# Six up projections of a two-block transformer as seven block products for eight

## The reference

```
h2 = rms_norm(x, norm2[l])
x = x + jnp.square(jax.nn.relu(h2 @ w_up[l])) @ w_down[l]
...
FFN_HIDDEN = math.ceil(8 * D_MODEL / 3 / 256) * 256
...
def swiglu_ffn(x, w_gate_up, w_down):
    gu = x @ w_gate_up
    gate, up = gu[..., :FFN_HIDDEN], gu[..., FFN_HIDDEN:]
    return (jax.nn.silu(gate) * up) @ w_down
```

## Time and profile before

| | us |
|---|---|
| median of 3 runs (2246.28 to 2247.21) | 2246.77 |
| the profiled execution | 2248.02 |
| its span, first to last instruction | 2246.3 |
| TensorE busy | 2184.9 |
| VectorE busy | 1036.7 |
| ScalarE busy | 842.4 |
| GpSimd busy | 243.5 |

### The profile page before, as it was taken

How to read it: one execution, slowest core, us unless ns; L and a number is a source line. 1 busy time by engine, 2 the same in 40 slices (tenths; PEclk the granted TensorE clock), 3 DMA queues, 4 the chain that set the end, 5 groups by cost and what they waited for, 6 DMA issues and landing times.

```text
span 2246.3 us, 34926 instructions
## 1 busy us (share of the span) xinstructions
PE 2184.9 (97%) x14575; PEld 1791.7 (80%) x14575; DVE 1036.7 (46%) x1704; ACT 842.4 (38%) x1480; POOL 243.5 (11%) x327
## 2 busy tenths in 40 slices
PE   8999999999999999988999999999999999999998
PEld 7777778888888887867878888888976779888887
DVE  5243436454344345556547443333535555333335
ACT  5354444342232235234334323222446644222231
POOL 4000000000000011102314100000422214000000
PEclk9999999999999999989999999999999999999999
DMA  5312123233333323200013233333232212333321
GB/s 171 85 57 57 48 67 103 85 94 94 99 98 94 85 86 85 76 21 2 3 30 100 83 115 94 96 96 100 69 82 67 71 47 83 106 103 103 93 86 65
DMA packets 341336, 179.65 MB, mean 80 GB/s; under 512 B 44151, under 2 KB 332069, under 8 KB 341181
## 3 DMA queue, kind: packets, MB, share of 16 engines
q1 hardware_dynamic: 338860, 171.54, 27.2%
q0 software_dynamic: 2320, 5.89, 0.9%
HBM read 172.40 MB, written 2.11 MB: 78 GB/s over the span
## 4 chain that ended last, share of the span: by engine, by line
PE 45%; DVE 2%; POOL 1%; ACT 1%; issue 1%; DMA 0%; DVEq 0%; POOLq 0%; ACTq 0%
PE bank L462 13%; PE bank L464 13%; PE bank L463 13%; PE bank L1405 2%; PE bank L1431 1%; PE bank L1417 1%; POOL x L1063 0%; ACT w_hi L438 0%; PE bank L923 0%; PE bank L2933 0%; POOL act_lo L972 0%; PE bank L2941 0%; DVE w_lo L445 0%; DMA mla_swapped<-mla_qr 0%; DVE o L967 0%
## 5 line engine op out<-in xcount | busy, mean ns | idle before, releaser
L462 PE MATMUL bank<-act_hi,w_hi 128*128 128x512 f32 (+1 forms) x1960 | 737.0, 376 | 10.5 <-DVE w_lo L445 3.3
L464 PE MATMUL bank<-act_hi,w_lo 128*128 128x512 f32 (+1 forms) x1960 | 714.6, 365 | 0.0
L463 PE MATMUL bank<-act_lo,w_hi 128*128 128x512 f32 (+1 forms) x1960 | 714.4, 364 | 0.0
L445 DVE TENSOR_TENSOR w_lo<-w,w_hi 128x1024 fp32r<-128x1024 f32 (+2 forms) x327 | 400.2, 1225 | 404.5 <-ACT w_hi L438 404.3
L438 ACT ACTIVATE w_hi<-w 128x1024 fp32r<-128x1024 f32 (+1 forms) x328 | 336.6, 1028 | 342.2 <-PE bank L464 326.6
L462 PEld LDWEIGHTS bank<-act_hi,w_hi 128*128 128x128 f32 x1960 | 370.7, 189 | 84.2 <-issue 17.5
L464 PEld LDWEIGHTS bank<-act_hi,w_lo 128*128 128x128 f32 x1960 | 370.7, 189 | 60.1
L463 PEld LDWEIGHTS bank<-act_lo,w_hi 128*128 128x128 f32 x1960 | 371.4, 190 | 53.7 <-issue 1.0
L462 PE MATMUL bank<-hid_hi,w_hi 128*128 128x512 f32 (+1 forms) x672 | 249.5, 371 | 0.0
L463 PE MATMUL bank<-hid_lo,w_hi 128*128 128x512 f32 (+1 forms) x672 | 247.9, 369 | 0.0
L464 PE MATMUL bank<-hid_hi,w_lo 128*128 128x512 f32 (+1 forms) x672 | 247.8, 369 | 0.0
(11 more groups left out here) (440 smaller groups left out, 2352.4 us busy)
## 6 DMA issues: line engine op xcount, KB each, us to landing
w<-in_ffn_w_gate_up SPq DMA_DIRECT2D x88, 512.0 KB, 3.8
w<-in_w_in SPq DMA_DIRECT2D x41, 512.0 KB, 3.8
w<-in_w_up SPq DMA_DIRECT2D x32, 512.0 KB, 4.0
w<-in_w_down SPq DMA_DIRECT2D x32, 512.0 KB, 3.8
w<-in_ffn_w_down SPq DMA_DIRECT2D x32, 512.0 KB, 3.9
w<-in_even_w_in SPq DMA_DIRECT2D x28, 512.0 KB, 3.8
w<-in_ffn_w_down SPq DMA_DIRECT2D x16, 384.0 KB, 3.4
w<-in_w_out SPq DMA_DIRECT2D x8, 512.0 KB, 3.9
```

The lines of the kernel that those rows point to most:

```text
L445: e.tensor_tensor(w_lo[:, 0:part.n], w.raw[part.g % w.LOADS][:, 0:part.n], w_hi[:, 0:part.n].bitcast(F32), ALU.subtract).then_inc(w.lo.sem, 1)
L462: e.matmul(s.acc, *first, start=(k == 0), stop=False)
L463: e.matmul(s.acc, *second, start=False, stop=False)
L464: last = e.matmul(s.acc, *third, start=False, stop=(k == kt - 1))
```

## The change

Six up jobs are computed by another rule: `up1`, `up2`, `up3` (squared ReLU) and `up01`, `up02`, `up11` (gated). Two tiles of output are taken as a pair. The pair's product is a matrix product of 2 x 2 blocks: the weight's blocks are a11, a12 (first tile, input features 0 to 511 and 512 to 1023), a21, a22 (second tile), the activation's are 512 features x 256 tokens, b11 to b22. Winograd's form of Strassen's rule needs seven block products where the plain one needs eight:

- sums of the activation, t1 = b12 - b11, t2 = b22 - t1, t3 = b22 - b12, t4 = b21 - t2, made once for each norm's result by GpSimd, split by ScalarE and VectorE (`scalar_after`, `vector_after`);
- sums of the weight, s1 = a21 + a22, s2 = s1 - a11, s3 = a11 - a21, s4 = a12 - s2, made for each pair by GpSimd, four additions of 128 x 512;
- seven products, each of 4 x 3 matmuls of 256 columns;
- results joined: ScalarE copies product 1 out of PSUM (`kept`), VectorE makes four additions with one input in PSUM, three of 512 columns and one of 256, into `z` in SBUF. The epilogue then reads `z` and not a bank, so its work on the pair's two tiles starts behind the fourth addition.

The weight parts of a pair are now a (a11, a12: 1024 columns), b (s2, s1), c (s3, s4) and d (a22, 512 columns), so four splits of 3584 columns in all where two of 2048 were. Loads stay two for a pair; the first buffer is free when the fourth sum and the split of a are made, the second when the split of d is made. In the jobs above TensorE runs 84 matmuls of 256 columns for a pair instead of 48 of 512; 36 pairs are changed.

The core of the diff:

```diff
+    def gpsimd(self, e):
...
+        s2, s1, s3, s4 = (self.S[:, n * T:(n + 1) * T] for n in range(4))
+        for s in self.subs:
+            pair, i = s.pair, s.pair.i
+            (a11, a12), (a21, a22) = pair.blocks()
+            if before:
+                e.wait_ge(*w.sums.at(4 * i))
+                e.wait_ge(*w.lo.at(before.parts[1].g + 1))
...
+            e.wait_ge(*w.landed_at(pair.loads[1]))
+            e.tensor_tensor(s1, a21, a22, ALU.add).then_inc(w.sums.sem, 1)
+            e.wait_ge(*w.landed_at(pair.loads[0]))
+            e.wait_ge(*w.sums.at(4 * i + 1))
+            e.tensor_tensor(s2, s1, a11, ALU.subtract).then_inc(w.sums.sem, 1)
+            if before:
+                e.wait_ge(*w.lo.at(before.parts[2].g + 1))
+            e.tensor_tensor(s3, a11, a21, ALU.subtract).then_inc(w.sums.sem, 1)
+            e.wait_ge(*w.sums.at(4 * i + 2))
+            e.tensor_tensor(s4, a12, s2, ALU.subtract).then_inc(w.sums.sem, 1)
+            before = pair
...
+        def product(acc, part, at, x):
...
+            w_hi, w_lo = g.split_of(part)
+            for k in range(4):
+                high, low = x(k)
+                cols = slice(at * T + k * P, at * T + (k + 1) * P)
+                e.matmul(acc, w_hi[:, cols], high, start=k == 0, stop=False)
+                e.matmul(acc, w_hi[:, cols], low, start=False, stop=False)
+                last = e.matmul(acc, w_lo[:, cols], high, start=False, stop=k == 3)
+            return last
...
+        e.wait_ge(*w.lo.at(a.g + 1))
+        room(0)
+        product(p1, a, 0, plain(0, first)).then_inc(w.made.sem, 1)
+        room(1)
+        product(p2, a, 1, plain(1, first)).then_inc(w.used.sem, 1)
+        e.wait_ge(*w.lo.at(b.g + 1))
+        product(p6, b, 0, sums(1)).then_inc(w.made.sem, 1)
+        room(2)
+        product(p5, b, 1, sums(0)).then_inc(w.used.sem, 1)
+        e.wait_ge(*w.lo.at(c.g + 1))
+        product(p7, c, 0, sums(2)).then_inc(w.made.sem, 1)
+        room(3)
+        product(p3, c, 1, plain(1, second)).then_inc(w.used.sem, 1)
+        e.wait_ge(*w.lo.at(d.g + 1))
+        product(p4, d, 0, sums(3)).then_inc(w.used.sem, 1)
+
+    def emptied(self, i, n):
+
+        w = self.w
+        return (w.kept.at(i + 1), w.added.at(4 * i + 1), w.added.at(4 * i + 3), w.added.at(4 * i + 4))[n]
...
+        e.wait_ge(*w.made.at(3 * i + 2))
+        e.wait_ge(*w.kept.at(i + 1))
+        e.tensor_tensor(z[:, 0:5:4, :], p2_p6, spread(self.kept[:, :], 2), ALU.add).then_inc(w.added.sem, 1)
+        for old in s.carried + [a]:
+            for part in g.next_of(old):
+                g.split_low(e, part)
+        e.wait_ge(*w.made.at(3 * i + 3))
+        e.wait_ge(*w.added.at(4 * i + 1))
+        e.tensor_tensor(z[:, 5:7, :], p5_p7, spread(z[:, 4, :], 2), ALU.add).then_inc(w.added.sem, 1)
+        e.wait_ge(*w.added.at(4 * i + 2))
+        e.tensor_tensor(z[:, 3, :], p5_p7[:, 0, :], z[:, 6, :], ALU.add).then_inc(w.added.sem, 1)
+        for part in g.next_of(b):
+            g.split_low(e, part)
+        e.wait_ge(*w.used.at(d.g + 1))
+        e.tensor_tensor(z[:, 1:3, :], p3_p4, z[:, 5:7, :], ALU.add).then_inc(w.added.sem, 1)
...
         for c, (first, n) in enumerate(CHUNKS):
...
+            if layer == 0 and c or layer and c == 1:
+                jobs[f"up{layer}{c}"] = SevenJob(w, f"up{layer}{c}", 2 * n, KD, pieces)
```

More of the change, by code:

```diff
@@ L235, in load, with loads_before @@
                 dst = dst.rearrange("p k (h n) -> p (k h) n", n=src.shape[-1])
[L236 to L242, removed]
+            e.dma_start(dst, src).then_inc(self.landed[n % self.LOADS].sem, 16)
+    def loads_before(self, e, n):
+        n = min(n, len(self.loads))
+        for i in range(self.issued, n):
+            self.load(e, i)
+        self.issued = max(self.issued, n)
 class Job:
@@ L273, in factors, with __init__, bind_seven, starts @@
         return (w_hi[:, at:at + P], hi), (w_hi[:, at:at + P], lo), (w_lo[:, at:at + P], hi)
+class SevenJob(Job):
+    def __init__(self, weights, name, tiles, kt, pieces):
+        self.name, self.tiles, self.kt, self.group = name, tiles, kt, 1
+        self.pairs = [weights.add_pair(kt, pieces(u), pieces(u + 1)) for u in range(0, tiles, 2)]
+        self.parts = [part for pair in self.pairs for part in pair.parts]
+    def bind_seven(self, seven):
+        self.seven = seven
+        for pair in self.pairs:
+            pair.seven = seven
+    def starts(self, u, k):
+        return None
+    def ends(self, u, k):
+        return None
 class TokenJob(Job):
@@ L359, in __init__ @@
             s.n, s.acc, s.before = n, self.bank[b][:, s.cols], before.get(b)
-            before[b] = s
+            if s.pair is None:
+                before[b] = lambda s=s: s.job.epilogue.emptied(self, s)
+            elif s.group:
+                four = [(n + i) % self.BANKS for i in range(4)]
+                s.banks, s.befores = [self.bank[b] for b in four], [before.get(b) for b in four]
+                for i, b in enumerate(four):
+                    before[b] = lambda s=s, i=i: s.job.seven.emptied(s.pair.i, i)
             found[s.job, s.u, s.cols.start, s.cols.stop] = s
@@ L369, in __init__ @@
                         part.ended_in = leader.n + -(-leader.group * (k + 1) // s.job.kt) - 1
-            if not s.ends[-1]:
+            if s.pair and s.group:
+                s.last = n + 2 == len(self.subs) or self.subs[n + 2].pair is None
+                s.carried = self.subs[n - 1].pair.parts[2:] if self.subs[n - 1].pair else []
+                for k, part in enumerate(s.pair.parts):
+                    part.ended_by, part.ended_in = n + 1 if s.last and k >= 2 else None, None
+            elif not s.pair and not s.ends[-1]:
                 partial += 1
@@ L495, in _ @@
             for s in self.subs:
-                if s.group:
+                if s.pair and s.group:
+                    s.job.seven.multiply(e, s, between)
+                elif s.group:
                     self.multiply(e, self.subs[s.n:s.n + s.group], between)
```

248 lines of the change are left out of this document (211 added, 37 removed).

## The result

The changed kernel takes 2269.2 us (median of 4 runs, 2268.49 to 2274.29), the kernel before 2247.0: 1.0101 times as long, 95% interval 1.0085 to 1.0117. The forecast was 2258, +11; it came to +22. The profiled execution is the longest of the four (2274.3, span 2272.3), so its parts add up to 26.0 us, not to 22.

What follows compares the result with a forecast made beforehand. TensorE's matmul columns bound the kernel while splits, sums and epilogues keep ahead. Three ReLU chunks at +2.0 and three gated at +1.6 give +10.8 on 2248.0, 1.3 less for the median: forecast 2258 us, range 2230 to 2276, its own 2250 to 2267.

Steps and rivals of the forecast that it cites:

- Matmuls at 0.12: On TensorE, 256-column matmuls start every 0.12 us, so seven products take 10.08 us against 10.88 before.
- The wait of 0.3 ahead of the second product: In gated pairs from the fourth on, TensorE gaps of about 0.3 us before product 2, released by a VectorE addition.
- Late: 1.75 - 0.9 = 0.85: In a gated pair, GpSimd holds VectorE 1.75 us against 0.9 slack, so the next pair's first product waits 0.85 us.
- The slack: In a gated pair, VectorE reaches add 3 in 4.9 us, TensorE needs it after 5.76: 0.9 us spare.
- the restart: After a gated pair's wait, TensorE loses 0.07 us more on starting again.
- The gated chunk: Up job of eight gated pairs: -1.6 + 5 x 0.55 - 0.5 + 0.9 = +1.6 us.
- the free pairs: First two pairs of a chunk save 0.80 us each, their sums being made during the down tiles.
- The hidden tile out late: Behind a chunk's last pair, the down job waits for the hidden tile: 0.9 us gated (0 to 1.5), ReLU 1.7.
- The ReLU chunk as a whole: Four pairs: two free (-1.6), third +2.4, last -0.5, hidden tiles 1.7 late: +2.0 us.
- The input sums at 0 to 3: Activation sums on GpSimd and their splits, during the up*0 jobs and first down tiles: 0, at most 3 us per stage.
- "The rest" at 0: Outside the chunks: input sums, load issue and GpSimd's later work were counted as adding 0.
- Rival C: GpSimd's chain of split, load and four additions sets the pair at 12.1 us: +25, total 2272; chance 0.17.

Runs made afterwards that it cites:

- last two narrow: Changed kernel with GpSimd's third and fourth weight sums cut to 8 of 512 columns from a stage's second pair on: 2234.9 us, ratio 0.9943.
- last-pair run: Changed kernel with the last pair of each of the six chunks computed as two plain tiles again: 2254.8 us, ratio 1.0027.
- first two pairs: Changed kernel with only the first two pairs of each of the six chunks as seven products, the rest plain: 2243.4 us, ratio 0.9986.
- ReLU chunks alone: Changed kernel with only the three squared ReLU chunks as seven products, the gated ones as before: 2259.3 us, ratio 1.0055.

## Why the prediction was wrong

The direction and most places were right, the size was not: +22.2 against +10.8, and the forecast's own range ended at 2267.

- **Matmuls at 0.12**: right, slightly better (9.96 for a pair against 10.08). First three gated pairs without a wait, waits from the fourth on, released by the third addition: right. The wait of 0.3 ahead of the second product is not there; small gaps stand in its place.
- **The step that failed is "Late: 1.75 - 0.9 = 0.85"** of the gated pair, forecast at 11.4 us, measured at 11.5 to 12.2, 11.85 on average over 15 pairs. Both terms were mis-sized. The slack was 0.51 and not 0.9: I left out hand-overs. The first joining addition starts 0.42 behind product 3's last matmul and not 0.2, and TensorE goes on 0.15 behind the third. The holds add up to 2.15 on average (1.7 to 2.4 in single pairs) and not 1.75, since I took the first two additions as free. In a pair on time they are (last two narrow: 9.96); in one that has waited the first can hold the epilogue's multiply (0.72 in the first pair shown), and where it does not, the last two hold the splits in full (2.35 in the next). Against these the restart costs 0.31, where 0.47 was counted (0.07, and 0.4 for the fourth addition). Average pair: 9.96 - 0.51 + 0.25 (the 0.31 in 12 pairs of 15, as a chunk's third pair starts on time) + 2.15 = 11.85.
- **The gated chunk**: the free pairs (-1.7 for two) and the last one (-0.5) came as forecast. The five pairs between are +5.15 in `up01` where 5 x 0.55 = 2.75 was counted. The three chunks are +2.95, +2.47 and +2.35, where the forecast's terms without the late hidden tile give +0.65.
- **The hidden tile out late**: gated 0.9 forecast, 1.3 to 1.4 measured; ReLU 1.7 forecast, 1.7 to 1.9 measured. The last-pair run shows its cause. The ReLU chunk as a whole: +2.0 forecast, +2.2 to +2.3 measured; its third pair takes 13.27 (13.3 forecast), its second 10.3 (counted as free).
- **The input sums at 0 to 3**: 1.9 in `down0`, value taken 0. In the trace the split of an input sum (1.14 us) and held instructions stand ahead of `up0`'s last low part; with them behind it, 1.9 went.
- **"The rest" at 0**: the recurrent stage got 3.6 us longer, for which I had no row. A stall of 2.4 us is in it; by the counts above the 72 more matmuls and weight loads of each pair in front of it moved a border of TensorE's instruction blocks there.
- **Rival C** had nearly the time (2272) for a wrong reason: at 12.1 per pair it named GpSimd's chain with the loads. With GpSimd as long at work the pair fell to 10.59.

The Trainium skill (Advanced Engine Details and Errata, GPSIMD Details) puts the conflict at VectorE instructions of two SBUF inputs or in a 2-port performance mode. The one-input `tensor_scalar` was held here as well (0.43 us alone, 1.23 beside an addition), which agrees with it if its short form is such a mode; no view here names the mode.

What stays open: why only some borders of TensorE's instruction blocks cost time in the recurrent stage (one of 2.4 us in the changed kernel, one of 0.41 with the ReLU chunks as before), and why a one-input GpSimd instruction holds less. Neither was tried. The 5 us by which the profiled run is above the other three are not placed either, as those have no trace.

## What to carry to other kernels

Before adding work on GpSimd, add up the time for which it and VectorE hold each other in a turn of the loop: here a gated pair asked 4.0 (splits) + 1.2 (epilogue) + 4 x 1.12 = 9.7 of 9.96 us, and only a perfect packing would have been free; the first two additions alone were, four cost 2. Such work is cheap at the start of a stage, where it falls beside a job with slack, so change the first pairs of a chunk and leave the last one, whose end somebody waits for. And count a chain in hand-overs from a trace, not only in durations: 0.4 us of slack that was not there is 6 us in 15 pairs, in a forecast that missed by 11.

## What was not expected of the hardware

- A VectorE `tensor_scalar` of 512 columns from SBUF to SBUF takes 0.43 us, and 1.23 beside a GpSimd addition.
- GpSimd with one input of 512 columns is no faster in these chunks than with two (1.49 to 1.74 us against 1.29 to 1.74), yet holds VectorE less: a split of 1024 columns takes 1.63 beside it, against 2.3 beside a sum of two inputs, and 1.22 alone.
- TensorE stalled 0.4 to 2.4 us at borders between blocks of its own instructions, in a stage of small matmuls: 19 times in 13 traces, all with the same remainder (193 or 194) when its recorded instructions are counted in 256s, and each until 1.2 to 1.6 us behind the landing of a block.
- A stall of 2.2 us left TensorE at 1.2 GHz for 21.7 us in one run (first two pairs), and at 2.4 GHz throughout in another (ReLU chunks alone, granted clock 1.00 in the 21.7 us behind it).
